# Expert weights loaded in pairs of chunks, 2 MB a transfer, in a hybrid attention and mixture-of-experts layer

## The reference

```
xn   = rms_norm(h);  proj = xn @ w_in                       # 1024 x (columns of both head groups)
h    = h + concat[gla(proj), diff_attention(proj)] @ w_out
x    = rms_norm(h)
g    = top-1 of 4 groups (softmax);  e = top-2 of its 8 experts, weights renormalized and scaled by g's
h    = h + sum over the 2 experts of weight * (silu(x @ w1[e]) * (x @ w3[e])) @ w2[e]
```

## Time and profile before

| | us |
|---|---|
| median of 3 runs | 1171.98 |
| lowest and highest | 1170.74 to 1173.13 |
| the profiled execution | 1173.08 |
| its span in the profile | 1171.3 |
| PE busy | 1116.4 (95%) |
| DVE busy | 882.4 (75%) |
| ACT busy | 692.8 (59%) |
| POOL busy | 335.6 (29%) |

### The profile page before, as it was taken

How to read it: one execution, slowest core, us unless ns; L and a number is a source line. 1 busy time by engine, 2 the same in 40 slices (tenths; PEclk the granted TensorE clock), 3 DMA queues, 4 the chain that set the end, 5 groups by cost and what they waited for, 6 DMA issues and landing times.

```text
span 1171.3 us, 17264 instructions
## 1 busy us (share of the span) xinstructions
PE 1116.4 (95%) x5838; PEld 860.8 (73%) x5839; DVE 882.4 (75%) x1326; ACT 692.8 (59%) x930; POOL 335.6 (29%) x394
## 2 busy tenths in 40 slices
PE   6999999999999989999699999999999999999997
PEld 5877887767777678888567777777777777777775
DVE  4424323666566787888679999999999999999995
ACT  5424202544455544435347777777777788888884
POOL 1211102321111222222463242323323245444211
PEclk9998999999999999999789999999999999999999
DMA  8130302110200264442589999999999999999993
GB/s 323 46 108 1 108 1 72 33 67 28 99 28 18 91 186 140 133 177 93 206 318 382 375 393 378 383 396 373 395 375 378 385 376 383 403 394 391 392 368 81
DMA packets 67327, 271.66 MB, mean 232 GB/s; under 512 B 13172, under 2 KB 19896, under 8 KB 42808
## 3 DMA queue, kind: packets, MB, share of 16 engines
q1 hardware_dynamic: 57000, 245.32, 54.0%
q0 software_dynamic: 6800, 19.14, 7.0%
q10 hardware_dynamic: 3456, 6.29, 1.4%
HBM read 248.44 MB, written 26.48 MB: 235 GB/s over the span
## 4 chain that ended last, share of the span: by engine, by line
PE 80%; DVE 10%; ACT 5%; POOL 2%; issue 2%; DMA 1%; ACTq 0%; POOLq 0%; DVEq 0%
PE main_pm L693 13%; PE main_score L693 7%; PE main_score L2083 5%; PE main_score L2085 5%; PE main_score L2084 5%; DVE main_w_low L2053 4%; PE main_score L754 3%; PE main_pt L2085 3%; PE main_po L2085 3%; PE main_pt L2083 3%; PE main_po L2083 3%; PE main_pt L2084 3%; PE main_po L2084 3%; ACT main_w_high L2049 2%; PE main_pt L2095 2%; PE main_po L777 2%
## 5 line engine op out<-in xcount | busy, mean ns | idle before, releaser
L2053 DVE TENSOR_TENSOR main_w_low<-w_raw,main_w_high 128x2048 fp32r<-128x2048 f32 x190 | 432.8, 2288 | 34.7 <-ACT main_w_high L2049 34.3
L2049 ACT CAST main_w_high<-w_raw 128x2048 fp32r<-128x2048 f32 x190 | 362.3, 1908 | 70.6 <-PE main_score L2085 54.1
L1952 POOL DMA_INDIRECT main_xg<-xn_dram,main_token x32 | 75.2, 2349 | 280.9 <-DVE main_token L1925 269.8
L2083 PE MATMUL main_score<-main_w_high,main_hT_high 128*96 128x512 f32 x256 | 102.7, 401 | 1.1 <-DVE main_hT_low L2340 0.5
L2085 PE MATMUL main_score<-main_w_high,main_hT_low 128*96 128x512 f32 x256 | 100.7, 393 | 0.0
L2084 PE MATMUL main_score<-main_w_low,main_hT_high 128*96 128x512 f32 x256 | 100.3, 392 | 0.0
L693 PE MATMUL main_pm<-slot_high,xh 128*128 128x512 f32 x208 | 87.7, 422 | 2.1 <-DVE slot_low L1404 2.1
L693 PE MATMUL main_pm<-slot_low,xh 128*128 128x512 f32 x208 | 83.0, 399 | 0.0
L693 PE MATMUL main_pm<-slot_high,xl 128*128 128x512 f32 x208 | 82.8, 398 | 0.0
L1997 POOL DMA_INDIRECT out<-main_y,main_dest x31 | 50.1, 1616 | 87.2 <-ACT main_y L2009 60.2
L1055 ACT ACTIVATE main_prob<-main_score,main_nmax 128x128 f32<-128x128 f32 (+7 forms) x64 | 47.5, 743 | 33.6 <-DVE main_nmax L1463 32.7
(11 more groups left out here) (374 smaller groups left out, 2621.9 us busy)
## 6 DMA issues: line engine op xcount, KB each, us to landing
w_raw<-in_moe_w SPq DMA_DIRECT2D x192, 1024.0 KB, 19.3
slot_raw<-in_w_in SPq DMA_DIRECT2D x12, 1024.0 KB, 7.2
main_x<-in_x SPq DMA_DIRECT2D x8, 512.0 KB, 11.2
slot_raw<-in_w_out SPq DMA_DIRECT2D x4, 1024.0 KB, 6.6
main_hx<-in_x SPq DMA_DIRECT2D x8, 512.0 KB, 4.0
out<-main_hx SPq DMA_DIRECT2D x8, 512.0 KB, 2.6
xn_dram<-main_xn SPq DMA_DIRECT2D x8, 512.0 KB, 2.9
gr_dram<-main_stage ACTq DMA_DIRECT2D x8, 256.0 KB, 2.0
```

Source lines behind the costliest of these rows:

```text
L1952: nc.gpsimd.indirect_dma_start(xg[u][:], None, s["xn2_dram"], bass.IndirectOffsetOnAxis(token[u][:, 0:1], 0), bounds_check=bound["x"], oob ...
L2049: nc.scalar.copy(wh[slot(c, e)][:], raw[u][c // 2][:, c % 2, :]).then_inc(w_high, 1)
L2053: nc.vector.tensor_tensor(wl[slot(c, e)][:], raw[u][c // 2][:, c % 2, :], wh[slot(c, e)][:].bitcast(F32), ALU.subtract).then_inc(w_low, 1)
L2083: nc.tensor.matmul(out, x_hi, w_hi, start=start, stop=False)
```

## The change

Two chunks of a matrix come with one transfer of 2 MB, with 16 KB for each partition, in place of two of 1 MB. SP's list of chunks is 0, 2, 4 in place of 0 to 5. The transfer for a pair is issued once the low part of the second chunk of that buffer is done, and both chunks' casts wait for its one semaphore. The last two transfers, of the tail, stay as they are. The first loads, in the front, are paired too, at the places of their first chunks. Buffers, casts, products and the software queue stay as they are.

```diff
@@ -389,7 +389,7 @@
 
     def first_high(act, c):
 
-        act.wait_ge(s["raw_in"][0][c], 16)
+        act.wait_ge(s["raw_in"][0][0], 16)
         nc.scalar.copy(w_first[0][c][:], s["raw_pair"][0][0][:, c, :]).then_inc(w_split_high, 1)
 
     def first_low(dve, c):
@@ -638,15 +638,12 @@
             if RING <= n + 2 < T:
                 load_tile(n + 2)
             elif n == RING + 3:
-                for c in range(2):
-                    load_chunk(sp, a, s, 0, 0, c, 0, None)
+                load_chunk(sp, a, s, 0, 0, 0, 0, None)
             elif n == T:
                 sp.wait_ge(g_o_mm, T)
-                for c in (0, 1):
-                    load_chunk(sp, a, s, 1, 1, c, 1, 0)
+                load_chunk(sp, a, s, 1, 1, 0, 1, 0)
                 sp.wait_ge(added, 2 * T - 1)
-                for c in (4, 5):
-                    load_chunk(sp, a, s, 0, 0, c, 0, None)
+                load_chunk(sp, a, s, 0, 0, 4, 0, None)
             sp.wait_ge(added, 2 * t + 2)
             sp.dma_start(h_rows[t], hx[:, t % 2, :]).then_inc(h_out[t % 2], 16)
             sp.wait_ge(normed, t + 1)
@@ -1818,14 +1815,13 @@
                      w[:, 2 * (c % 2):2 * (c % 2) + 2, :]).then_inc(s["raw_in"][u][c], 16)
         return
     w = expert_weights(a, ("moe_w1", "moe_w2", "moe_w3")[c // 2], before if c in (2, 3) else which)
-    sp.dma_start(s["raw_pair"][u][c // 2][:, c % 2, :], w.rearrange("p (c k) f -> p c (k f)", c=2)[:, c % 2, :]) \
+    sp.dma_start(s["raw_pair"][u][c // 2][:].rearrange("p c x -> p (c x)"), w.rearrange("p k f -> p (k f)")) \
         .then_inc(s["raw_in"][u][c], 16)
 
 
 def chunks_of(e):
 
-    return (2, 3) if isinstance(e, int) and e == NE else (0, 1, 4, 5) if isinstance(e, int) and e == 0 \
-        else range(CHUNKS_E)
+    return (2, 3) if isinstance(e, int) and e == NE else (0, 2, 4)
 
 
 def stage_experts(nc, a, s, tools, front):
@@ -2035,7 +2031,10 @@
 
     def high(act, e, r, u, c):
 
-        act.wait_ge(raw_in[u][c], 16 * (r + u) if c in (2, 3) else 16 * (r + 1))
+        if isinstance(e, int) and e == NE and c == 3:
+            act.wait_ge(raw_in[u][3], 16)
+        else:
+            act.wait_ge(raw_in[u][c // 2 * 2], 16 * (r + u) if c in (2, 3) else 16 * (r + 1))
         n = number(e, c)
         if isinstance(e, int) and e == 0:
             if c == 4:
@@ -2070,10 +2069,10 @@
         which = None if tail else ranked(sp, e)
         before = ranked(sp, e - 1)
         for c in chunks_of(e):
-            if isinstance(e, int) and e == 2 and c in (2, 3):
+            if isinstance(e, int) and e == 2 and c == 2:
                 sp.wait_ge(chunk_used, 4)
             else:
-                sp.wait_ge(w_low, number(e - 2, c) + 1)
+                sp.wait_ge(w_low, number(e - 2, c if tail else c + 1) + 1)
             load_chunk(sp, a, s, e, j % 2, c, which, before)
 
     def ranked(eng, e):
@@ -2466,7 +2465,7 @@
     def sync(sp):
         for u in range(2):
             sp.wait_ge(q.xg_in[u], 16)
-        for chunk in (2, 3, 4, 5):
+        for chunk in (2, 4):
             load_chunk(sp, a, s, 1, 1, chunk, 1, 0)
         over_experts(sp, sp_expert)
 
@@ -2527,7 +2526,7 @@
 
     parked, turn = sem("parked"), sem("turn")
     starts, shift, o_gated, o_down = listed, hT_low, chunk_used, list_mm
-    o_w_in, loaded = [raw_in[0][c] for c in (0, 1, 4)], 16 * (NE // 2)
+    o_w_in, loaded = [raw_in[0][c] for c in (0, 2, 4)], 16 * (NE // 2)
     o_xT, o_hT = xT_high, hT_high
 
     class o:
```

## The result

The changed kernel takes 1225.9 us (median of 4 runs, 1225.61 to 1230.59) where the kernel before took 1172.56 beside it (4 runs, 1170.74 to 1173.18): a ratio of 1.047, interval 1.0452 to 1.0488, so 53 us slower. The forecast was 1196 with a range up to 1222. The sign holds, and so does the wait through which the loss was to come; the size is twice what was worked out and outside the range, because this wait has a second effect, on POOL, that was not in the sum.

What follows compares the result with a forecast made beforehand. The prediction took the kernel as bound by PE, then DVE, with transfers right behind. Waits for scatters added 18 us in heavy and 6 in light experts, 24 on the median of 1171.98: 1196 us, range 1172 to 1222.

Steps and rivals of the forecast that it cites:

- the wait through which the loss was to come: DVE writes a list's weights (L1931) only after an earlier scatter lands; 2.3 us to spare in heavy experts, 2.5 in light.
- the sum: Added delay through DVE's wait for scatters: 18 us in heavy experts plus 6 in light ones, 24 us, bounds +9 to +50.
- First step: On the loads' queue q1, packets become 16 KB long and fall by about 12,200.
- Rival C: Gather and scatter each wait for one turn of a load's whole share, 2.5 us longer: about 1220 us; chance 0.05.
- Second step: Beside 16 KB load records, heavy experts' gathers land after about 11.6 us and scatters after about 13.
- the joint landing: A pair's first half lands with its second, 2.5 us late for a cast in late light experts: 0 to 2.5 us.
- Rival B: Hidden anyway: rows cut into 8 KB pieces or turns by bytes, only joint landing left: 1172 to 1174.5 us; chance 0.23.
- D: Faster: fewer, longer records raise the loads' rate; 7 us, 1165, were the transfers the bound; chance 0.06.
- E: Worse: PE's waits let its clock fall, as from 580 to 600 us; over 1222 us; chance 0.05.
- Third step: Later landings exceed the 2.3 us to spare, so DVE idles some 1 to 2 us per expert before L1931.
- the ring: Late L1931 delays next gather, scatter and L1931: 1.4 us per heavy expert, 0.6 per light; rival A, 1196 us, chance 0.61.
- What limits this: DVE's waiting shortens the 13 us load queue; once gone, gather and scatter meet free engines: heavy part 25 us cut to 18.

Runs made afterwards that it cites:

- a8: Kernel before with the loads' records cut to 4 KB (products not the reference's, for time only): 1171.75 us, 1.0002.
- a6: Kernel before with each pair as two 1 MB transfers of 16 KB records, even and odd partitions, with the pair's timing: 1213.8 us, 1.0354.
- a5: Kernel before with the pair's timing alone: two 1 MB loads of 8 KB records issued after the second low part, casts waiting for both: 1174.6 us, 1.0025.
- a3: Changed kernel with DVE's wait for the scatter moved behind its last low part of the expert: 1175.6 us, 1.0038 to the kernel before.
- a7: Changed kernel where DVE, in written-out experts, waits behind its first low part until POOL has issued the gather: 1203.2 us, 1.0273 to the kernel before.
- b3: Changed kernel with the two loops over experts written out: 1340.3 us (2 runs), 1.144 to the kernel before.
- b4: Kernel before with its two loops over experts written out: 1173.3 us, 1.0034.
- a4: Kernel before with DVE's wait for the scatter moved behind its last low part of the expert: 1174.3 us, 1.0024.
- a2: Kernel before with each pair as two 1 MB transfers of 16 KB records, each to 64 adjacent partitions, casts waiting for both: 1451.4 and 1523.0 us.
- a1: Changed kernel with the 2 MB transfer's pattern written as two runs of 8 KB in each partition: 1216.8 and 1238.0 us.

## Why the prediction was too low

**First step, 16 KB records: right.** The packets fell by what was said. Where a gather runs beside loads (after, 661 to 664.5 us):

```profile
q1 hardware_dynamic: 60, 0.95, 64.8%
q0 software_dynamic: 62, 0.25, 36.2%
```

60 packets, less two of a few bytes, are 58 records of 16 KB in 36.3 engine-us (64.8% of 16 x 3.5), 0.63 us each, beside 62 of 4 KB of 0.33. A turn of the loads costs 0.63 for the 0.31 of before, and the queues still go record by record, near one to one. Rival C, turns of a whole share, falls.

**Second step, later landings: right.** 11.6 and 13 us were forecast for heavy experts, 12.0 and 13.7 came. a8, a6 and a5 make it cause and not company: it goes with the record, and not with the transfer or the joint landing, which cost 2.5 us (a5), the upper bound. Rival B falls, as does D (4 KB records, twice as many, cost nothing: a8). E falls too: the granted clock fell only to 0.98 and 0.94 in the two stretches, for 1.00 in both the earlier trace rows, and the waits that set the period are DVE's.

**Third step, the ring: right in kind, and in size partly by luck.** The sum had 18 us for 18 heavy experts, 1.0 each, after the limit; the heavy loop lost 1.0 for each. It had 0.6 for a light one; 0.7 came. By the table above, all that stands outside the six intervals with a long gather is 18 us (10.7, 6.2 and 1.0); 24 were forecast for all experts. But the sum left out two things that work against each other: the 1.2 us that a gather can be late before the scatter is (1.5 us of idle time before, 0.3 after), and that single scatters of the heavy loop land after up to 15.2 us, not after 13.

**"What limits this": wrong.** "Once it is gone, gather and scatter meet free engines." The queue of loads did shrink, from 13 us (18.4 less 5.0 for a load alone) to 4 (10.7 less the 6.8 of the shortest), but the landings did not get shorter with it. As I read it, a landing is that of the slowest of 16 engines, and some of them are never free. After, from 916 to 919 us, the ends of a scatter still stand beside a full queue of loads:

```profile
q1 hardware_dynamic: 78, 1.25, 97.0%
q0 software_dynamic: 13, 0.02, 4.2%
```

The step took the heavy ring from 25 to 18 us, which came out right in number for a reason that isn't shown; its real harm was to cap the upper bound of the range.

**The failed step is the sum's list of terms.** It followed the delay from DVE over POOL to the scatter with POOL's instructions at a fixed price (2.27 and 1.63 us). That fixed price is the step that failed. The missing term is what the wait does to POOL: DVE gets behind ACT, so that its low parts no longer have to wait for casts, and it runs without the gap of 0.44 us; the gather's instruction then takes 7.5 to 10.4 us in place of 2.3, the scatter behind it is late by that, and the next wait is long. It cost 35.1 us in six experts by the table, of which about 6 (an estimate: 1.0 each, as in the loop) would have come by the ring anyway. The term that the sum had at nothing is thus about 29 of the 53 us. The chain is shown by taking out one link at a time: no wait, no new long gather and 4 us of loss (a3); a gap in DVE, no long gather and 22 us back (a7); written-out code everywhere, long gathers everywhere (b3); the same code without the wait, none (b4).

The row that could have warned stood in the trace of before: one gather of 8,128 ns over a median of 2,267, in an expert that is written out. I had read the medians. The median itself was a sign as well, since a gather with DVE idle takes 1.03 us.

The Trainium skill, page SBUF — State Buffer, section Who interferes with whom, says that DVE and GpSimd share a port pair by an exclusive lock, and that a `tensor_tensor` with both inputs in SBUF contends with a GpSimd instruction that reads SBUF. The trace fits this in the loops: the gather at 903.33 takes 2.26 us and ends 0.87 us after the first of two low parts that follow each other without a gap. It differs in written-out code: the page has the lock for one instruction, 2.28 us here, and at 641.18 POOL was held over the rest of one and six more, until DVE's first gap.

Open: why POOL gets in between DVE's instructions in the loops and not in written-out code. The effect is shown (b3 against the changed kernel), its cause is not. Register work between a loop's instructions is a guess that no run tried by itself. That a lock on a port is what holds POOL is not shown either; the runs show only that its instruction ends behind a low part and, in written-out code, needs a gap. Open too are the 0.2 to 0.4% that a3, a4, a5 and b4 cost.

## What to carry to other kernels

The length of a load's row is the price of a turn for every small transfer that shares the DMA engines with it. Where a shorter row has the same rate (4 and 8 KB here, 383 and 384 GB/s) and nobody waits for the loads, a longer one buys nothing and makes gathers and scatters late.

When a change brings a wait within reach of zero spare time, look at what the waiting engine does afterwards. Work that has been held back runs without gaps, and an engine that needed those gaps may be held up. Read the longest of a group beside its median; and where a wait has no spare time, place it behind the work that doesn't need it (a3 took nearly all of the loss away without touching a transfer).

## What the runs showed of the hardware that was not expected

- POOL's instruction that issues a gather takes 1.03 us with DVE idle (before, 601.27) and 2.3 us when it begins beside one of DVE's fp32 subtractions of 128x2048. In written-out code, beside an unbroken row of DVE's instructions, it takes 7.5 to 10.4 us. It ends some 0.9 us after a subtraction does, in the second case after the last one ahead of a gap (650.63 and 651.54). A gap of 0.44 us was enough (before at 641.01, b4 at 656.10).
- A transfer to 64 adjacent partitions has about half the rate, 230 GB/s with the engines at a share of 1.02 (a2). Transfers to 64 alternate ones have all of it, 437 GB/s (a6).
- Two runs of 8 KB that are adjacent on both sides travelled as one record of 16 KB, though the pattern names them as two (a1: 43,320 packets, as with one run).
- A third of the pairs in 16 KB records delays a gather nearly as much as all of them (11.8 us for 12.0; 9.7 without). That fits a landing that waits for the slowest of 16 engines, but no run tried it by itself.
